# Forty-four modulation tiles moved to row products beside the up projections, and the inverse's transposes moved to VectorE

## The chip, the core and the metric

The kernel runs on one core of a Trainium2 chip. The metric is device time in microseconds (us): the median of several runs of the whole program. The engines are PE (TensorE), DVE (VectorE), ACT (ScalarE), POOL (GpSimd) and SP (SyncE, which issues most transfers); each works through its own list of instructions in order, and semaphores hold them to each other.

## What is computed

Two transformer-like blocks run one after the other on 256 tokens of width 1024, all in 32-bit floats. Cut to what matters here:

```python
def first_block(x, p, ...):                    # 256 x 1024
    z = rmsnorm(h) @ mix_w_in                  # layer 0
    y_a = rwkv7_bidir(z[..., :RWKV_COLS])      # 8 heads of 64, two directions, a recurrence over time
    y_b = hyena_bidir(z[..., RWKV_COLS:])      # long convolution by DFT products
    h = h + concat([y_a, y_b]) @ mix_w_out
    h = h + conv_ffn(h); h = h + per_layer_embedding(h)
    h = h + neighbourhood_attention(...)       # layer 1
    h = h + conv_ffn(h); h = h + per_layer_embedding(h)

def conv_ffn(h):
    u = dwconv_centred(rmsnorm(h) @ w_up, conv_w, conv_b)      # 1024 -> 2 x 2816
    return (gelu(u[..., :D_FF]) * u[..., D_FF:]) @ w_down

def second_block(x, c, ctx, c_ctx, w_mod, b_mod, ...):         # x is the first block's result
    for l in range(2):
        ml = split(silu(c) @ w_mod[l] + b_mod[l], 9)           # w_mod[l] is 1024 x 9216
        mc = split(silu(c_ctx) @ w_mod[l] + b_mod[l], 9)
        ...                                                    # half FFN, mixing, half FFN, modulated by ml, mc
```

The **modulation** of the second block depends on `c` and `c_ctx` alone, not on the first block: 2 layers x 9216 columns, for two conditions, that is 144 tiles of 128 columns (36 blocks of 512). It can be worked out at any time before the norms that use it.

## The kernel before

The stages follow each other on PE: in-projection of the first block (to about 121 us), hyena (121 to 167), the low-rank products of the RWKV ("lora", 167 to 187), its recurrence (187 to 369), the out-projection, the first conv FFN (up projection 408.6 to 560.8, down projection to about 633), embedding and neighbourhood attention, the second conv FFN (up projection from about 841), and from then on the second block (half00, mix0, half01, half10, mix1, half11).

**The modulation by PE.** 21 of the 36 blocks (all 18 of layer 0, the last three of layer 1) are computed as matrix products in small pieces that other stages let in. `tensor_modulation`, `scalar_modulation` and `vector_modulation` are generators; `Fill.to(n)` runs one of them up to step n, so that its instructions stand at that place of the engine's list. Block j takes two steps: step 2j+1 is the first eight products of 512 weights columns, step 2j+2 the second eight, with a small product ("columns", 128x4) that turns block j-1 ahead of them. The banks 2 and 3 of the PSUM alternate, so PE's step 2j+1 waits until DVE has done `add(j-2)` (L888), which stands in DVE's step 2j; PE's columns wait for a copy by ACT. Of the 43 steps 14 stand in the hyena (`HY_FILL` gives those between its DFT products: up to step 6, 8 and 12 after products 3, 5 and 7), two in the lora stage (`MOD_EARLY`, 16), and seven in each of the four recurrences (`fill_at`).

**The modulation by rows.** The other 60 tiles, all of layer 1, are computed by DVE without PE, 20 in each of half00, half01 and half10: a tile of 128 rows x 1024 of the transposed weights is loaded by an ACT queue (`scalar_rows_load`), and DVE multiplies it by silu(c) and silu(c_ctx) and adds up along the row, one instruction each (`vector_row`, L1354); `vector_rows_bias` adds the bias at the end. Two tile buffers alternate.

**The recurrence.** `tensor_scan`, `scalar_scan` and `vector_scan` run once for each of four pairs of heads, p = 0 to 3. In chunks of 64 steps the recurrence needs the inverse of a triangular matrix for eight units. It is built by doubling blocks, in levels 1 to 5 (block sizes 4 to 64): with `xi` the inverse so far and `xt` its transpose, PE computes p = et' xi, ACT copies it to `pk` (L1074), PE computes the correction dx = xt' pk and also dt = pk' xt, and DVE subtracts dx from xi (L1120) and dt from xt (L1124); level 5 has dt alone. Before level 1, xt is made by DVE (L1106), PE transposes it by products with the identity into bank `b0` ("xit"), and DVE copies that to xi (L1109). DVE fills its time between with the operands of the next pair, one piece in each level (`vector_prepare`, lines 730 to 775); p = 3 has no next pair. After the levels each p has a tail of products of the outputs and the state, with fills at points 13 to 18.

**The conv FFN.** `scalar_norm` lets ACT square the input, load the table with the logarithm (L269) and form 1/rms; `vector_norm` scales, and the up projection runs over 22 pairs (f) of column tiles of two halves: per half PE fills a bank, ACT takes the middle tap (`mid_tap`), DVE adds the outer two, and per f ACT's gelu and a DVE product end it. In the last four f DVE also forms sums of weights for the down projection (`vector_weight_sums`). `vector_fast` then forms the sums of activations (L1524) with which the down projection's fast scheme goes on.

All products of PE go through the helper at line 134; `sb_work`, `sb_big`, `sb_xn`, `sb_rope` are large on-chip buffers cut into areas, `weights` is a ring of four slots, `acc` and `aux` are four PSUM banks each.

## Time and profile before

| what | us |
|---|---|
| runs | 3063.7, 3064.5, 3067.2; median 3064.5 |
| span of the profiled execution | 3064.9 |
| PE busy | 2938.8 (96%) |
| DVE busy | 1524.0 (50%) |
| ACT busy | 594.4 (19%) |
| chain of waits, share of PE | 88% |

PE is busy nearly all the time, and it is also what the chain that ended last runs through: what leaves PE's list where PE is the bound is gained. The stages around the change are the exceptions to look into: between 121 and 370 us PE waits more often than elsewhere. A timeline row gives start and length in us, the engine, line, operation, the tiles out<-in, and how many records are put together; in brackets the idle time of the engine ahead of it and who ended it. One instruction of the program on a pair of halves shows as two records.

### The profile page before, as it was taken

What the parts mean: (1) busy time and instruction counts of PE and PEld (TensorE: products, weight loads), DVE (VectorE), ACT (ScalarE), POOL (GpSimd) and SP (SyncE); (2) the same over time, 40 slices, a digit from 0 to 9 for tenths busy, and PEclk for the clock granted to TensorE, in tenths of its full rate; (3) what the DMA queues carried; (4) which work ended last, traced back from release to release, by engine and by line L of the source; (5) the groups of instructions that cost most, each with busy time, mean ns of one, the idle gap of its engine ahead of it and who ended that gap; (6) DMA issues with size and microseconds to landing.
All of it is one profiled execution on the core that took longest, in us unless ns stands there. A gap on an engine that the chain in (4) does not pass through costs nothing.

```text
span 3064.9 us, 42878 instructions
## 1 busy us (share of the span) xinstructions
PE 2938.8 (96%) x17846; PEld 2394.0 (78%) x17846; DVE 1524.0 (50%) x3105; ACT 594.4 (19%) x1355; POOL 37.3 (1%) x60
## 2 busy tenths in 40 slices
PE   9988899999899999999999899999999999999999
PEld 7666788987588978888843448888878888765999
DVE  4266433532534556665313736666366673225675
ACT  1233222122422030100112621100020000224110
POOL 0000000020000000000000000000000000000000
PEclk9999999999999999999999999999999999999999
DMA  6644444465243544332303023332344322331444
GB/s 240 235 165 167 146 141 137 125 202 156 76 147 113 165 145 144 130 92 77 128 15 93 28 82 115 126 110 80 93 143 139 116 78 76 112 106 45 149 140 109
DMA packets 349316, 374.15 MB, mean 122 GB/s; under 512 B 8163, under 2 KB 282996, under 8 KB 348612
## 3 DMA queue, kind: packets, MB, share of 16 engines
q1 hardware_dynamic: 336228, 329.72, 34.3%
q10 hardware_dynamic: 10688, 36.38, 3.5%
q0 software_dynamic: 2208, 5.31, 0.9%
q8 instruction: 143, 2.34, 0.3%
q14 instruction: 49, 0.40, 0.0%
HBM read 370.34 MB, written 1.05 MB: 121 GB/s over the span
## 4 chain that ended last, share of the span: by engine, by line
PE 88%; DVE 6%; ACT 4%; issue 2%; DMA 0%; ACTq 0%; DVEq 0%
PE acc L134 74%; PE aux L134 13%; ACT sb_xn L280 1%; PE aux L2283 1%; ACT L269 0%; DVE sb_work L2009 0%; DVE sb_work L2006 0%; DVE sb_work L1519 0%; ACT sb_work L1808 0%; ACT sb_work L1810 0%; DVE sb_xn L258 0%; DVE sb_big L1120 0%; DVE sb_work L2020 0%; ACT sb_rstd L271 0%; DVE sb_work L1788 0%
## 5 line engine op out<-in xcount | busy, mean ns | idle before, releaser
L134 PE MATMUL acc<-sb_xn,weights 128*128 128x256 f32 (+2 forms) x5184 | 1215.6, 389 | 20.5 <-DVE sb_xn L258 12.2
L134 PEld LDWEIGHTS acc<-sb_xn,weights 128*128 128x128 f32 x5184 | 946.5, 191 | 243.8 <-issue 123.2
L134 PE MATMUL acc<-sb_work 128*128 128x256 f32 (+1 forms) x1944 | 374.7, 346 | 0.0
L134 PEld LDWEIGHTS acc<-sb_work 128*128 128x128 f32 x1944 | 324.3, 191 | 34.3 <-issue 0.4
L134 PE MATMUL acc<-sb_work,weights 128*128 128x256 f32 (+2 forms) x1508 | 322.5, 362 | 3.2 <-DVE sb_work L1257 1.4
L134 PE MATMUL acc<-sb_big,weights 128*128 128x256 f32 (+1 forms) x1776 | 315.4, 334 | 4.3 <-DVE sb_work L1667 4.0
L134 PEld LDWEIGHTS acc<-sb_big,weights 128*128 128x128 f32 x1776 | 279.7, 192 | 31.0 <-issue 5.7
L134 PEld LDWEIGHTS acc<-sb_work,weights 128*128 128x128 f32 x1508 | 254.5, 191 | 50.2 <-issue 21.8
L1487 ACT COPY sb_work<-acc 128x256 f32<-128x256 f32 (+1 forms) x112 | 37.9, 339 | 687.1 <-PE acc L134 687.1
L134 PE MATMUL aux<-sb_xn,sb_work 128*128 128x256 f32 (+1 forms) x704 | 152.2, 361 | 8.9 <-ACT sb_xn L280 8.9
L1557 DVE TENSOR_TENSOR sb_work<-sb_work,acc 128x256 f32<-128x256 f32 (+1 forms) x112 | 42.6, 380 | 226.5 <-PE acc L134 226.5
L1519 DVE TENSOR_TENSOR sb_work<-weights 128x512 f32<-128x512 f32 (+1 forms) x112 | 99.7, 890 | 95.2 <-PE acc L134 95.0
L1492 ACT ACTIVATE sb_work<-sb_work 128x256 f32<-128x256 f32 (+1 forms) x88 | 34.4, 391 | 570.7 <-DVE sb_work L1571 570.7
L134 PEld LDWEIGHTS aux<-sb_xn,sb_work 128*128 128x128 f32 x704 | 124.2, 195 | 24.3 <-issue 10.2
L1665 DVE SCALAR_TENSOR_TENSOR sb_work<-acc,sb_cols,sb_work 128x255 f32<-128x255 f32 x88 | 42.5, 482 | 187.3 <-ACT sb_work L1652 187.3
L134 PE MATMUL aux<-sb_big,sb_work 128*128 128x128 f32 (+3 forms) x592 | 110.9, 342 | 0.0
L1519 DVE TENSOR_TENSOR weights<-weights 128x512 f32<-128x512 f32 (+1 forms) x112 | 99.7, 890 | 3.1
L1519 DVE TENSOR_TENSOR sb_work<-sb_work,weights 128x512 f32<-128x512 f32 (+1 forms) x112 | 99.2, 886 | 2.6
L1599 DVE TENSOR_TENSOR sb_work<-sb_work,acc 128x256 f32<-128x256 f32 (+1 forms) x112 | 42.5, 379 | 116.2 <-PE acc L134 116.1
L1519 DVE TENSOR_TENSOR sb_work<-weights,sb_work 128x512 f32<-128x512 f32 (+1 forms) x112 | 99.1, 885 | 0.7
L134 PEld LDWEIGHTS aux<-sb_big,sb_work 128*128 128x128 f32 (+1 forms) x592 | 89.2, 186 | 10.9 <-issue 2.8
L1571 DVE TENSOR_TENSOR sb_work<-sb_work,aux 128x256 f32<-128x256 f32 (+1 forms) x112 | 42.4, 379 | 104.2 <-PE aux L134 104.2
(316 smaller groups left out, 2709.5 us busy)
## 6 DMA issues: line engine op xcount, KB each, us to landing
weights<-ffn_w_up SPq DMA_DIRECT2D x88, 1024.0 KB, 7.9
weights<-ffn_w_down SPq DMA_DIRECT2D x48, 1408.0 KB, 7.2
weights<-ffn_w_gate SPq DMA_DIRECT2D x44, 1024.0 KB, 5.4
weights<-w_mod SPq DMA_DIRECT2D x21, 2048.0 KB, 8.2
sb_work<-w_mod_rows ACTq DMA_DIRECT2D x60, 512.0 KB, 6.4
weights<-w_in SPq DMA_DIRECT2D x8, 2048.0 KB, 8.6
weights<-mix_w_in SPq DMA_DIRECT2D x6, 2048.0 KB, 12.7
weights<-na_w_qkv SPq DMA_DIRECT2D x6, 2048.0 KB, 10.8
```

The costliest lines, as they stand in the source:

```text
L134: return te.matmul(o, lhsT, rhs, start=start, stop=stop, skip_group_check=True)
L280: shifted.on(ac.activation(y, y, ACT.Identity, bias=N.shift(k, h)))
L1487: st_u.on(ac.copy(u[:, s, :], bank_a[:, 0:F.H]))
L1492: st_g2.on(ac.activation(g2[:, s, :], g2[:, s, :], ACT.Silu))
L1519: st_s.on(ve.tensor_tensor(to, one, other, op))
L1557: st_b.on(ve.tensor_tensor(u, u, bank_b[:, 0:F.H], ALU.add))
L1571: st_c12.on(ve.tensor_tensor(g2, g2, bank_e[:, 0:F.H], ALU.add))
L1599: st_c21.on(ve.tensor_tensor(u, u, bank_c[:, 0:F.H], ALU.add))
L1665: v_step.on(ve.scalar_tensor_tensor(u[:, 1:L], ps[:, 0:L - 1], cols("ffn_cw", 1, 132 * F.i + t), u[:, 1:L], ALU.mult, ALU.add))
L2283: ins_ = te.transpose(aux[u % 3][:, c:c + 128], mx_e[:, u % 4, W * i + 128 * kt:W * i + 128 * kt + 128], ident[:])
```

## The change

1. 11 of the 21 blocks leave PE: `MOD_BY_PE` keeps blocks 16 and 17 of layer 0 and 0 to 5, 16 and 17 of layer 1. Of the 21 steps left, two stand at the hyena's start and up to step 4 after its transposes, up to 9 after the last DFT product, 11 after the inverse, 13 in the lora stage, 14 to 16 ahead of the first recurrence, and one each of 17 to 21 in the recurrences (two in p = 3).
2. 44 more tiles go by rows: tiles 0 to 21 of layer 0 beside the first conv FFN's up projection, 22 to 43 beside the second's, with three tile buffers of their own. ACT issues the load of the conditions (1 MB) and of three tiles inside the norm, between the squares and the table load, after a wait for the whole input; it then takes the Silu and goes on as before, with a load in each f from 2 on. DVE does one row product per half and the bias after the last. The half FFNs keep 20 tiles each, now 44 to 63 of layer 0 and 24 to 63 of layer 1.
3. In the recurrence DVE transposes 32 x 32 blocks in place of PE: xi from xt before level 1 (the 32 small products of "xit" and the copy L1109 go), and xt from the new xi in levels 1 to 4 (dt's 16 instructions and the subtraction L1124 go). Up to there the inverse is zero outside of blocks of 32. Level 5 keeps dt.

The core of the diff:

```diff
+MOD_BY_PE = [(0, 16), (0, 17)] + [(1, b) for b in (0, 1, 2, 3, 4, 5, 16, 17)]
...
-    def scalar_norm(N):
+    def scalar_norm(N, between=None):
...
+        if between is not None:
+            between()
         ac.preload_act_table_set(NAT_LOG)
...
-    HY_FILL = {3: 6, 5: 8, 7: 12}
+    HY_FILL = {7: 9}
...
     def vector_hyena(other):
...
-        other.to(8)
+        other.to(4)
         ve.wait_ge(hy_spec.sem, hy_spec_at(7))
...
-        other.to(10)
+        other.to(6)
...
-        other.to(12)
+        other.to(9)
...
-    MOD_STEPS, MOD_EARLY = n_mod * 2 + 1, 16
+    MOD_STEPS, MOD_EARLY, MOD_FIRST = n_mod * 2 + 1, 13, 16
 
     def fill_at(p, point):
-        return min(MOD_STEPS, MOD_EARLY + 7 * p + point * 7 // 18)
+        return MOD_FIRST + (18 * p + point) * (MOD_STEPS - MOD_FIRST) // (18 * NP)
...
         other.to(fill_at(p, 2))
-        te.wait_ge(sc_xt.sem, sc_xt_at(p))
         te.wait_ge(sc_tm.sem, sc_tm_at(4 * p))
-        for u, hp, g, tt in UNITS:
-            for par in range(2):
-                ins_ = mm(b0[half(par), 64 * u:64 * u + 64], xt[half(par), u, :], ident[half(par), half(par)])
-        sc_xit.on(ins_)
...
                 sc_dx.on(ins_)
-            for u in range(8):
-                for par in range(2):
-                    ins_ = mm(aux[0][half(par), 64 * u:64 * u + 64], pk[half(par), u, :], xt[half(par), u, :])
-            sc_dt.on(ins_)
+            else:
+                for u in range(8):
+                    for par in range(2):
+                        ins_ = mm(aux[0][half(par), 64 * u:64 * u + 64], pk[half(par), u, :], xt[half(par), u, :])
+                sc_dt.on(ins_)
...
+        sc_xi.on(ve.transpose(wide(xi), wide(xt)))
         other.to(fill_at(p, 2))
-        ve.wait_ge(sc_xit.sem, sc_xit_at(p))
-        sc_xi.on(ve.tensor_copy(xi, blocks(b0[:])))
...
                 sc_xi.on(ve.tensor_tensor(xi, xi, blocks(aux[3][:]), ALU.subtract))
-            ve.wait_ge(sc_dt.sem, sc_dt_at(n))
-            if lv > 1:
+                ve.wait_ge(sc_xi.sem, sc_xi.n)
+                sc_xu.on(ve.transpose(wide(xt), wide(xi)))
+            else:
+                ve.wait_ge(sc_dt.sem, sc_dt_at(p))
                 ve.wait_ge(sc_xu.sem, sc_xu.n)
-            sc_xu.on(ve.tensor_tensor(xt, xt, blocks(aux[0][:]), ALU.subtract))
+                sc_xu.on(ve.tensor_tensor(xt, xt, blocks(aux[0][:]), ALU.subtract))
...
         for n, _ in enumerate(vector_prepare(0)):
-            if n == 1:
-                other.to(MOD_EARLY)
+            if n in (1, 2, 3):
+                other.to((MOD_EARLY, MOD_EARLY + 1, MOD_FIRST)[n - 1])
...
+    conv_cond, conv_tile = area(big, FT * L, 2, D), [area(big, FT * L + 2 * D + D * n, D) for n in range(3)]
...
-        scalar_norm(F.norm)
+        sig, value = F.norm.x_ready[KT - 1]
+        ac.wait_ge(sig.sem, value)
+        scalar_norm(F.norm, lambda: scalar_rows_begin(F.rows))
+        scalar_rows_cond(F.rows)
         for n, g in enumerate(F.groups):
             f, half = divmod(n, 2)
             t, u = f + half * FT, conv_u[:, f % 2, half, :]
+            if half == 0 and 2 <= f < ROWS_CONV - 1:
+                scalar_rows_load(F.rows, f + 1)
...
                     vector_weight_sums(F.fast, FT, (f - FT + 4,))
+            vector_row(F.rows, f, half)
+        vector_rows_bias(F.rows)
         vector_fast(F.fast, following=following)
```

PE's list in the hyena, from the DFT products of which two are left over (`aux<-sb_work 128x512`, two instructions each) to the inverse (`128x256 x16`); the products of weights are the modulation's steps, eight each, and `128x4 x2` its columns. Before:

```order
L134 MATMUL aux<-sb_work 128x512 x4
L134 MATMUL acc<-weights,sb_work 32x256 x8
L134 MATMUL acc<-sb_work,sb_rstd 128x4 x2
L134 MATMUL acc<-weights,sb_work 32x256 x8
L134 MATMUL aux<-sb_work 128x512 x4
L134 MATMUL acc<-weights,sb_work 32x256 x8
L134 MATMUL acc<-sb_work,sb_rope 128x4 x2
L134 MATMUL acc<-weights,sb_work 32x256 x16
L134 MATMUL acc<-sb_work,sb_rstd 128x4 x2
L134 MATMUL acc<-weights,sb_work 32x256 x8
L134 MATMUL aux<-sb_work 128x256 x16
```

Changed:

```order
L135 MATMUL aux<-sb_work 128x512 x16
L135 MATMUL acc<-weights,sb_work 32x256 x8
L135 MATMUL acc<-sb_work,sb_rope 128x4 x2
L135 MATMUL acc<-weights,sb_work 32x256 x16
L135 MATMUL acc<-sb_work,sb_rstd 128x4 x2
L135 MATMUL acc<-weights,sb_work 32x256 x16
L135 MATMUL aux<-sb_work 128x256 x16
```

The steps that stood between the DFT products are gone, and one run of steps stands between the last of these and the inverse, the last of them the first half of a block (step 9).

PE's list from the lora products (`aux<-sb_work 128x256`) over the norms of the first pair (`128x512`) to the first products of the recurrence (`64x128 x32`) and what follows them. Before:

```order
L134 MATMUL aux<-sb_work 128x256 x8
L134 MATMUL acc<-weights,sb_work 32x256 x8
L134 MATMUL acc<-sb_work,sb_rstd 128x4 x2
L134 MATMUL acc<-weights,sb_work 32x256 x8
L134 MATMUL aux<-sb_work 128x256 x4
L134 MATMUL acc<-sb_work,sb_blk 128x512
L134 MATMUL aux<-sb_work 128x256 x4
L134 MATMUL acc<-sb_work,sb_blk 128x512
L134 MATMUL aux<-sb_work 64x128 x32
L940 MATMUL acc<-sb_ident,sb_work 128x128 x8
L940 MATMUL aux<-sb_ident,sb_work 128x128 x8
L134 MATMUL acc<-sb_ident,sb_big 64x64 x16
```

Changed:

```order
L135 MATMUL aux<-sb_work 128x256 x8
L135 MATMUL acc<-sb_work,sb_rstd 128x4 x2
L135 MATMUL acc<-weights,sb_work 32x256 x16
L135 MATMUL aux<-sb_work 128x256 x4
L135 MATMUL acc<-sb_work,sb_blk 128x512
L135 MATMUL aux<-sb_work 128x256 x4
L135 MATMUL acc<-sb_work,sb_blk 128x512
L135 MATMUL acc<-sb_work,sb_rope 128x4 x2
L135 MATMUL acc<-weights,sb_work 32x256 x16
L135 MATMUL acc<-sb_work,sb_rstd 128x4 x2
L135 MATMUL acc<-weights,sb_work 32x256 x8
L135 MATMUL aux<-sb_work 64x128 x32
```

Step 13 now ends the run between the lora products 0 to 3 and 4 to 7, steps 14 to 16 stand ahead of the recurrence's first products, and the transposes "xit" (`acc<-sb_ident,sb_big 64x64 x16`) have no counterpart behind.

DVE's list at the start of the levels of p = 0 (the second row ahead of the first level's L743 is the xi copy, or the transpose in its place). Before:

```order
L1106 TENSOR_TENSOR sb_xn<-sb_big 128x512
L1109 COPY sb_big<-acc 128x512
L1115 TENSOR_TENSOR sb_xn<-sb_big 128x512
L743 SCALAR_TENSOR_TENSOR sb_work<-sb_work 128x256 x2
L745 TENSOR_TENSOR sb_work<-sb_work 128x512
L733 TENSOR_TENSOR sb_work<-sb_big 128x512
L736 SCALAR_TENSOR_TENSOR sb_work<-sb_work,sb_cols,sb_big 128x256 x2
L1120 TENSOR_TENSOR sb_big<-sb_big,aux 128x512
L1124 TENSOR_TENSOR sb_big<-sb_big,aux 128x512
L888 TENSOR_TENSOR sb_mod<-acc,sb_cols 128x2x2x2
```

Changed:

```order
L1108 TENSOR_TENSOR sb_xn<-sb_big 128x512
L1109 STREAM_TRANSPOSE sb_big<-sb_big 128x512
L1116 TENSOR_TENSOR sb_xn<-sb_big 128x512
L749 SCALAR_TENSOR_TENSOR sb_work<-sb_work 128x256 x2
L751 TENSOR_TENSOR sb_work<-sb_work 128x512
L739 TENSOR_TENSOR sb_work<-sb_big 128x512
L742 SCALAR_TENSOR_TENSOR sb_work<-sb_work,sb_cols,sb_big 128x256 x2
L1121 TENSOR_TENSOR sb_big<-sb_big,aux 128x512
L1123 STREAM_TRANSPOSE sb_big<-sb_big 128x512
L1116 TENSOR_TENSOR sb_xn<-sb_big 128x512
```

The number of DVE's instructions in a level stays; the copy from a bank and the second subtraction, which waited for PE, are transposes of what DVE itself has written just before.

## Rows read from the trace of the kernel before

**Rows 1.** Busy time by stage: stretch, length, PE, PEld, DVE, ACT, POOL, clock, DMA share, GB/s

```profile
187.60:370.00 182.40, 154.94 (x3846) 126.30 (x3847) 110.66 (x214) 50.23 (x106) 0.00 (x0) 0.98 0.45 152
408.00:561.00 153.00, 152.19 (x704) 133.84 (x704) 58.23 (x118) 34.86 (x67) 0.00 (x0) 1.00 0.42 130
```

**Rows 2.** Chain of waits in the hyena: start, length, engine, tile, line, count

```profile
136.44 2.54 PE acc L134 x36
```

**Rows 3.** Timeline, hyena: start, length, engine, line, operation, count, [idle before, releaser]

```profile
153.28 1.07 PE L134 MATMUL acc<-weights,sb_work 128*32 128x256 f32 x16 [1.96 <-DVE sb_mod L888]
```

**Rows 4.** Timeline, low-rank stage and the first recurrence's start

```profile
173.75 1.07 PE L134 MATMUL acc<-weights,sb_work 128*32 128x256 f32 x16
176.51 0.16 DVE L888 TENSOR_TENSOR sb_mod<-acc,sb_cols 128x8 f32<-128x8 f32 x1
183.64 0.69 DVE L766 TENSOR_TENSOR sb_work<-sb_work 128x512 f32<-128x512 f32 x1 [4.00 <-ACT sb_work L807]
187.64 3.69 PE L134 MATMUL aux<-sb_work 64*64 64x128 f32 x64 [6.82 <-DVE sb_work L774]
```

**Rows 5.** Timeline, third recurrence (p = 2): start and first level

```profile
283.59 1.98 PE L134 MATMUL aux<-sb_work 64*64 64x128 f32 x64 [1.15 <-DVE sb_work L1153]
289.21 0.68 DVE L1109 COPY sb_big<-acc 128x512 f32<-128x512 f32 x1
290.81 1.15 PE L134 MATMUL aux<-sb_big,sb_xn 64*64 64x64 f32 x32
292.73 1.10 PE L134 MATMUL aux<-sb_rope,sb_big 64*64 64x64 f32 x32
296.78 1.15 PE L134 MATMUL aux<-sb_big,sb_xn 64*64 64x64 f32 x32 [0.48 <-DVE sb_big L1120]
297.97 0.69 DVE L1115 TENSOR_TENSOR sb_xn<-sb_big 128x512 f32<-128x512 f32 x1 [0.58 <-PE aux L134]
```

**Rows 6.** Timeline, fourth recurrence (p = 3): three level starts, end of levels

```profile
336.97 1.15 PE L134 MATMUL aux<-sb_big,sb_xn 64*64 64x64 f32 x32
348.44 1.15 PE L134 MATMUL aux<-sb_big,sb_xn 64*64 64x64 f32 x32
352.21 1.15 PE L134 MATMUL aux<-sb_big,sb_xn 64*64 64x64 f32 x32
360.78 1.85 PE L134 MATMUL acc<-sb_xn,sb_big 64*64 64x128 f32 x29 [0.79 <-DVE sb_big L1124]
```

**Rows 7.** Chain of waits in the recurrence: fills, and a stall of issue

```profile
220.08 1.00 PE acc L134 x16
227.56 1.54 PE acc L134 x20
272.36 2.74 issue
```

**Rows 8.** Busy time in one stretch of level products (as Rows 1)

```profile
276.00:278.00 2.00, 2.00 (x31) 0.83 (x23) 0.75 (x2) 0.00 (x0) 0.00 (x0) 0.51 0.04 12
```

**Rows 9.** Timeline, first products of the two down projections

```profile
562.76 2.69 PE L134 MATMUL acc<-sb_big,weights 128*128 128x128 f32 x22 [2.00 <-DVE sb_work L1667]
997.25 4.21 PE L134 MATMUL acc<-sb_big,weights 128*128 128x128 f32 x22 [2.00 <-DVE sb_work L1667]
```

**Rows 10.** Timeline, DVE and PE just after the first up projection

```profile
564.31 1.62 DVE L1524 TENSOR_TENSOR sb_xn<-sb_big 128x1408 f32<-128x1408 f32 x1
566.07 2.69 PE L134 MATMUL acc<-sb_xn,sb_work 128*128 128x128 f32 x22 [0.62 <-DVE sb_xn L1524]
```

**Rows 11.** Timeline, what ACT issues and loads before a projection

```profile
838.72 1.28 ACT L269 ACT_TABLE_LOAD   x1
1110.08 1.03 ACTq L1335 DMA_DIRECT2D sb_work<-w_mod_rows  x2
```

**Rows 12.** Row products: busy, mean ns | idle; their loads: KB, us to landing

```profile
L1354 DVE SCALAR_TENSOR_TENSOR sb_work<-sb_work 128x1024 f32<-128x1024 f32 x60 | 73.1, 1218 | 0.1
sb_work<-w_mod_rows ACTq DMA_DIRECT2D x60, 512.0 KB, 6.4
```

More of the change, by code:

```diff
@@ L529, in tensor_hyena @@
             hy_inv.on(ins_)
-        other.to(14)
+        other.to(11)
     def vector_hyena(other):
@@ L556, in vector_hyena @@
             hy_out.on(ve.tensor_tensor(yb[:, ct, :], s_fm[:, ct, :], uhy[:, ct, :], ALU.mult))
-        other.to(14)
+        other.to(11)
     def scalar_hyena(other):
@@ L603, in scalar_lora @@
         wad_tanh.on(ac.activation(wad[0:64], wad[0:64], ACT.Tanh))
-        other.to(14)
+        other.to(11)
         for b in range(2):
@@ L700, in blocks, with wide @@
         return ap.rearrange("p (u t) -> p u t", u=8)
+    def wide(ap):
+        return ap.rearrange("p u t -> p (u t)")
     def quads(ap):
@@ L815, in tensor_prepare @@
         if p:
-            te.wait_ge(sc_xi.sem, sc_xi_at(5 * (p - 1)))
+            te.wait_ge(sc_tm.sem, sc_tm_at(4 * (p - 1)))
         q = t0 if p else dd
@@ L826, in tensor_prepare @@
         yield
-    mod_blocks = [(l, b, block(1, banks=(2, 3))) for l, b in [(0, b) for b in range(18)] + [(1, b) for b in range(BY_ROWS // 4, 18)]]
+    mod_blocks = [(l, b, block(1, banks=(2, 3))) for l, b in MOD_BY_PE]
     n_mod = len(mod_blocks)
@@ L1157, in tensor_recurrence @@
             pass
+        other.to(MOD_FIRST)
         for p in range(NP):
@@ L1165, in scalar_recurrence @@
             pass
+        other.to(MOD_FIRST)
         for p in range(NP):
@@ L1319, in build, with __init__ @@
     row_junk = area(big, 20 * T2, D)
+    conv_cond, conv_tile = area(big, FT * L, 2, D), [area(big, FT * L + 2 * D + D * n, D) for n in range(3)]
+    conv_junk = area(work, 3072, D)
     cond_in, cond_set = signal("row_condition_arrived", 16), signal("row_condition_set")
[L1321 removed]
+    rows_in, rows_done = [signal(f"mod_rows_arrived{n}", 16) for n in range(3)], signal("mod_rows_done")
     class ModRows:
[L1324 to L1325 removed]
+        def __init__(self, first, n=ROWS_EACH, cond=row_cond, tiles=row_tile, junk=row_junk):
+            self.first, self.n, self.silu_cond, self.tiles, self.junk = first, n, cond, tiles, junk
             self.cond, self.silu = cond_in.reserve(1)(0), cond_set.reserve(1)(0)
[L1327 to L1328 removed]
+            m = len(tiles)
+            at = [rows_in[i].reserve(len(range(i, n, m))) for i in range(m)]
+            self.arrived = lambda t: (rows_in[t % m], at[t % m](t // m))
             self.done = rows_done.reserve(2 * n)
     def scalar_rows_load(R, t):
[L1332 to L1333 removed]
+        m = len(R.tiles)
+        if t >= m:
+            ac.wait_ge(rows_done.sem, R.done(2 * (t - m) + 1))
         n0 = 128 * (R.first + t)
[L1335 removed]
+        rows_in[t % m].on(ac.dma_start(R.tiles[t % m], ins["w_mod_rows"][n0:n0 + 128, :]))
     def scalar_rows_begin(R):
[L1338 to L1339 removed]
+        cond_in.on(ac.dma_start(R.silu_cond.rearrange("p s k -> p (s k)"), ins["cond_rows"]))
+        for t in range(len(R.tiles)):
             scalar_rows_load(R, t)
@@ L1343, in scalar_rows_cond @@
         ac.wait_ge(cond_in.sem, R.cond)
-        cond_set.on(ac.activation(row_cond, row_cond, ACT.Silu))
+        cond_set.on(ac.activation(R.silu_cond, R.silu_cond, ACT.Silu))
     def vector_row(R, t, s):
@@ L1353, in vector_row @@
             ve.wait_ge(rows_done.sem, R.done(2 * t))
-        rows_done.on(ve.scalar_tensor_tensor(row_tile[t % 2] if s else row_junk, row_tile[t % 2], 1.0, row_cond[:, s, :],
-                                             ALU.mult, ALU.mult, accum_out=mod[:, 72 + R.first + t, s:s + 1]))
+        row = R.tiles[t % len(R.tiles)]
+        rows_done.on(ve.scalar_tensor_tensor(row if s else R.junk, row, 1.0, R.silu_cond[:, s, :],
+                                             ALU.mult, ALU.mult, accum_out=mod[:, R.first + t, s:s + 1]))
     def vector_rows_bias(R):
-        ve.wait_ge(rows_done.sem, R.done(2 * ROWS_EACH - 1))
-        m = mod[:, 72 + R.first:72 + R.first + ROWS_EACH, :]
-        v_step.on(ve.tensor_tensor(m, m, cols("b_mod", ROWS_EACH, 72 + R.first).unsqueeze(2).to_broadcast([128, ROWS_EACH, 2]), ALU.add))
+        ve.wait_ge(rows_done.sem, R.done(2 * R.n - 1))
+        m = mod[:, R.first:R.first + R.n, :]
+        v_step.on(ve.tensor_tensor(m, m, cols("b_mod", R.n, R.first).unsqueeze(2).to_broadcast([128, R.n, 2]), ALU.add))
     class Fast:
@@ L1628, in __init__ @@
             self.fast = Fast(CTX, up=False, hid_at=lambda f: (hid_set, hid(f)))
+            self.rows = ModRows(ROWS_CONV * i, ROWS_CONV, conv_cond, conv_tile, conv_junk)
             self.x_ready = self.fast.x_ready
@@ L2706, in layout @@
     arrays["w_ukv"] = np.concatenate([flat(ukv[..., 0:NOPE]), flat(ukv[..., NOPE:])], axis=-1)
-    arrays["w_mod_rows"] = a["w_mod_2"][1].T[0:128 * BY_ROWS]
+    arrays["w_mod_rows"] = a["w_mod_2"].transpose(0, 2, 1).reshape(DEPTH * 9 * D, D)
     arrays["cond_rows"] = np.broadcast_to(np.concatenate([a["c_ctx_2"].reshape(-1), a["c_2"].reshape(-1)]), (128, 2 * D))
```

24 lines of the change are left out of this document (7 added, 17 removed).

## The prediction

> **What bounds the kernel now.** I read the chain of waits first, then busy time by stage, then the timeline of PE and DVE. PE is busy 96% of the span and carries 88% of the chain, so an instruction that leaves PE is gained only where nothing else ends last. In the recurrence PE is busy 154.9 of 182.4 us and DVE 110.7; in an up projection PE 152.2 of 153.0 and DVE 58.2 [rows 1]. So the row products go where DVE is two thirds idle, and what they replace leaves a stage in which PE and DVE take turns: part of that work fills PE's waits today. In the first level of p = 2 PE's next product waits for DVE's L1120, not for PE's own list [rows 5]; in p = 3, where DVE prepares nothing, level follows level at PE's pace [rows 6]. So p = 0 to 2 are bound by DVE in levels 1 to 4, p = 3 by PE throughout.
>
> **The change part by part**, against the profiled span of 3064.9, which is 0.4 over the median.
>
> *Hyena.* Two groups of two steps between the DFT products are on the chain, 2.54 each, the first of them shown [rows 2]: **-5.1**. What is left, steps 5 to 9 after the last DFT product, has a new wait. Step 9 needs `add(2)`, which DVE now does only after the spectrum product that also releases the inverse. Before, such a wait for L888 cost 1.96 in this place [rows 3]. The inverse then waits for an add (0.16), some 0.3 of hand-over and a step of 1.07 [rows 4], less what the other steps covered: **+1.2**, and +0.2 for step 11 behind the last output product.
>
> *Low-rank stage.* Step 13 stood free at 173.75. Now it needs `add(4)`, which on DVE is queued behind the pieces of `vector_prepare(0)` where before an add stood at 176.51; PE comes to it at about 176.8, and behind it in PE's list stand the lora products 4 to 7 and the norm of p = 0. ACT reads these, and DVE waits 4.00 for ACT at 183.64 [rows 4], so all of it is on the path: **+3.0**. Steps 14 to 16 lie in the 6.82 that PE waits ahead of the recurrence and cost nothing there (1.54 each at most, rows as in [rows 7]). They keep PE busy: the first products took 3.69 after that wait, 1.98 in p = 2 [rows 4, 5]. Gain 0 to 1.7; I take **-0.5**, since PE still waits some 3 us there.
>
> *Starts of the recurrences.* The copy L1109 begins at 289.21 and level 1 at 290.81, behind fills and the product it waits for [rows 5]. DVE's transpose can start where the copy did (the row before it on DVE is the same) and takes, as I assume, the copy's 0.68: level 1 at 289.95, a gain of 0.85. In p = 3 the same reckoning gives 0.2. **-2.3** for four. No row shows a DVE transpose. Its bounds are 0.16, the shortest DVE row here [rows 4], and 1.218 for 1024 columns, the longest of one pass [rows 12]; I take 0.68, a copy of the same tile. The Trainium skill's "Vector Engine (DVE) Microarchitecture Reference", section 3.8 "The reshape front-end and per-opcode configuration", says the transpose mode sustains one element per cycle per lane, the rate of a plain copy; no run here shows it.
>
> *Levels 1 to 4 of p = 0 to 2.* PE loses dt (1.10), DVE swaps a subtraction for a transpose. After L1120 DVE has L1124 (0.68), then waits 0.58 for PE's product before L1115 [rows 5]; so the transpose is hidden up to about 1.2 us. The cycle of L1120, p, L1115 and the pieces of the next pair remains: **0**.
>
> *Levels of p = 3.* They took 360.78 - 336.97 = 23.8. One without a fill took 352.21 - 348.44 = 3.77 [rows 6]. Without dt PE could be faster still, but p, ACT's copy, dx and the subtraction follow each other in any case; 5 x 3.77 = 18.9. **-4.9**.
>
> *Level 5 and the tails of p = 0 to 2.* Nine fills of 1.00, 1.54 or (one) 1.76 are on the chain, 11.9 in all, the first two shown [rows 7]. Three of the new steps, some 3.0 together, come back there; of the other 8.9 a third is lost again because the copy or the subtraction behind a fill is late next: **-5.8**. A stall of issue of 2.74 on the chain [rows 7] follows a stretch in which the fills' loads saturate the transfers; their loads are gone: **-2.7**.
>
> *PE's clock.* After that stall the level products ran at a granted clock of 0.51, that is at 1.2 GHz [rows 8], and 22 products took 4.21 instead of 2.69 after an idle time of 2.00 that in the other down projection left the clock alone [rows 9]. Of eight idle times of 1.6 to 2.8 us in this trace, five show such a fall. Taking fills and dt away makes more: from the end of dx (292.73 + 1.10) to 296.78 PE had dt and a fill, and now has nothing for 2.9 us [rows 5]. I count twelve such turns of levels (four in each of p = 0 to 2) and four tails. A level product at 1.2 GHz costs 1.1 more (1.15 to 2.2). PE's slowness falls on the path in the turn of p, and partly under DVE's pieces in that of dx. Five eighths of 16 is 10, at 0.7 each: **+7** (0 to 17.6).
>
> *Up projections.* DVE: 58.2 + 44 x 1.218 [rows 12] = 111.8 of 153 us, and PE gives 152.2/22 = 6.92 per f for the two products. A tile lands in 6.4 [rows 12], three are in flight: hidden. Ahead of the table load ACT now issues four transfers, two of which took 1.03 [rows 11]: about 2. In the first conv FFN most lies under the wait for the last square, +0.7; in the second the table load at 838.72 [rows 11] is on the chain, +1.5. At the end the last row product (1.22) and the bias stand ahead of L1524, for which PE waits at 566.07 [rows 10]: +1.5 twice. **+5.2**, and **+1.5** (0 to 3.4) for the clock, since PE's idle 2.00 there grows [rows 9].
>
> **Sum**: -5.1 + 1.4 + 3.0 - 0.5 - 2.3 - 4.9 - 5.8 - 2.7 + 7 + 5.2 + 1.5 = -3.2. 3064.9 - 3.2 - 0.4 = 3061.3, so **3061**.
>
> **The rivals.**
>
> *The clock holds.* If nearly all 16 gaps are too short to lower it (as after the 2.00 of 562.76 [rows 9]), the +7 and the +1.5 go: 3061.3 - 8.5 = 3053. For it: three of eight gaps had no fall, and the gaps here recur with products between. Against: five of eight had.
>
> *Every gap lowers it* (the slower side). Then the twelve turns and four tails cost 1.1 each, 17.6 instead of 7: 3061.3 + 10.6 = 3072. The rest of the sum is -10.2, so this is slower than before from 10 us of clock cost, and clearly so from 17. For it: [rows 8], where a whole stretch stays low after one gap. The Trainium skill, "TensorE: Matmul & The Clock Gate", section "A second HAM failure mode: psum-queue depth-cycling", describes this: a TensorE that idles briefly between groups of products often enough swings between its two levels, and the loss is between the products rather than in them. The trace agrees in that the fall is at 272 us, after idle time between groups, not in a long run of products.
>
> *The transpose is slow.* At T us it costs 16 x (T - 1.2) in the levels and 4 x (T - 0.68) at the starts. At 1.8 that is 14: 3075. Slower than before from about 1.26, by more than can be told from no change from 1.56. For it: no row shows the operation; against: DVE's rows of 512 columns took 0.68 or 0.69, whatever they did [rows 4, 5].
>
> *The tails give it back.* If the nine fills only lie where DVE or ACT is next late by as much, -5.8 becomes -1: 3066.
>
> **How the numbers follow.** Forecast 3061 (its own range 3057 to 3066): 0.57. Clock holds, 3053 (3048 to 3057): 0.27. Every gap lowers it, 3072: 0.06. Slow transpose, 3075: 0.05. Tails give back, 3066: 0.05. The range 3050 to 3068 leaves out a fifth of the second case (0.05) and the two slow ones (0.11). A measurement of this kernel tells about 0.2%, 6.1 us, from no change: faster means below 3058.4, slower above 3070.6. Faster: the second case and a fifteenth of the first, 0.31; slower: the two slow cases less their near ends, 0.09; same: the rest, 0.60.
>
> **What would show it.** After: no steps between the DFT products, the inverse waiting a step longer; lora products 4 to 7 about 3 us later against the first ones; level 1 about 0.7 behind the copy's old place; STREAM_TRANSPOSE near 0.68; levels of p = 3 at 3.8 each, those of p = 0 to 2 as before (the first of p = 2 took 296.78 - 290.81 = 5.97 [rows 5]); the granted clock of the recurrence below the 0.98 of now [rows 1], with level products of 2.2 instead of 1.15; an up projection of 152.2, with its start and its end about 1.5 later against the stages around. The prediction is wrong where the transpose takes over 1.3, where the clock doesn't fall or falls throughout, where the recurrence is held by ACT instead, or where a row product ends later than its f.

## The result, and the profile after

The changed kernel takes **3067.3 us** (median of 20 runs, 3063.6 to 3071.1) against 3063.5 before (20 runs, 3059.3 to 3067.2). The ratio is 1.0014, 95% interval 1.0008 to 1.0020: some 4 us slower, where 3 us faster was forecast. By the forecast's bound of 0.2% it counts as the same; the time lies inside the range, but it went the other way. Runs of one kernel differ by some 8 us, and a profile is one of them; so kernels are compared by their medians, and profiles stage by stage.

The page of the changed kernel: busy time, and the granted clock in 40 slices of 77 us.

```profile
PE 2910.4 (95%) x16810; PEld 2375.2 (78%) x16810; DVE 1624.5 (53%) x3272; ACT 596.8 (19%) x1348; POOL 37.3 (1%) x60
...
PEclk9988899999999999999999999999999999999999
```

PE lost 28 us of busy time, DVE gained 100, and the time did not fall. The 8s in the clock line stand where the recurrences are. Busy time by stage (stretch, length, PE, PEld, DVE, ACT, POOL, granted clock, DMA share, GB/s): p = 0, 1 and 2, then the first up projection, which answer to [rows 1].

```profile
187.00:234.40 47.40, 32.70 (x700) 27.06 (x701) 32.01 (x60) 12.56 (x26) 0.00 (x0) 0.82 0.16 60
234.40:281.10 46.70, 32.74 (x704) 27.23 (x705) 30.99 (x57) 12.85 (x27) 0.00 (x0) 0.81 0.15 47
281.10:329.70 48.60, 32.45 (x704) 27.78 (x704) 30.91 (x56) 12.55 (x26) 0.00 (x0) 0.82 0.01 2
...
404.00:557.00 153.00, 152.18 (x704) 133.67 (x704) 106.72 (x204) 37.89 (x69) 0.00 (x0) 1.00 0.62 209
```

The granted clock of the recurrences was 0.98 over all four before; in three of them it is now 0.81 or 0.82, as a mean of stretches at 2.4 and at 1.2 GHz. In the up projection the row products are hidden, as forecast: DVE 106.7 (111.8 worked out), PE 152.2 as before.

PE's timeline in p = 0, first level to second, with the end of the levels:

```profile
193.50 1.15 PE L135 MATMUL aux<-sb_big,sb_xn 64*64 64x64 f32 x32 [2.56 <-DVE sb_big L1109]
194.45 1.13 PE L135 MATMUL acc<-sb_xn,sb_big 64*64 64x64 f32 x32
195.38 1.13 PE L135 MATMUL aux<-sb_rope,sb_big 64*64 64x64 f32 x32
199.45 1.97 PE L135 MATMUL aux<-sb_big,sb_xn 64*64 64x64 f32 x32 [2.94 <-DVE sb_big L1121]
201.35 2.07 PE L135 MATMUL acc<-sb_work,sb_blk 128*128 128x512 f32 x2
203.36 1.97 PE L135 MATMUL aux<-sb_rope,sb_big 64*64 64x64 f32 x32
...
222.24 3.46 PE L135 MATMUL acc<-sb_xn,sb_big 64*64 64x128 f32 x29 [0.79 <-DVE sb_big L1127]
```

Where dt and a fill stood [rows 5], PE waits 2.94 for DVE; the next product takes 1.97 instead of 1.15, and the ones behind it are as slow. The granted clock of that stretch is 0.50, that is 1.2 instead of 2.4 GHz:

```profile
198.70:205.50 6.80, 5.88 (x66) 4.07 (x66) 5.19 (x11) 2.21 (x4) 0.00 (x0) 0.50 0.00 1
```

PE stays there for several groups, not for one. The product behind the levels takes 3.46 where p = 3 of before took 1.85 [rows 6].

DVE at the same place:

```profile
192.69 0.70 DVE L1109 STREAM_TRANSPOSE sb_big<-sb_big 128x512 f32<-128x512 f32 x1
...
198.72 0.68 DVE L1121 TENSOR_TENSOR sb_big<-sb_big,aux 128x512 f32<-128x512 f32 x1
199.43 0.71 DVE L1123 STREAM_TRANSPOSE sb_big<-sb_big 128x512 f32<-128x512 f32 x1
201.47 0.69 DVE L1116 TENSOR_TENSOR sb_xn<-sb_big 128x512 f32<-128x512 f32 x1 [1.32 <-PE aux L135]
```

A transpose takes 0.70 to 0.71 (0.68 was assumed), and DVE then waits 1.32 for PE's slow product: it is not the transpose that holds the turn.

By stage, from the start of the first row of each to that of the next (us). The last column is the same stage in an experiment below that takes the cause away, or holds the clock by dead products. The hyena is an exception: no edit touches it, and the clock simply held there in e3, e7 and e8 (26.76 or 26.77); with the same instructions it took 28.1 to 29.8 in e2, e5, e6 and e10.

| stage | before | changed, two profiles | cause removed or clock held |
|---|---|---|---|
| hyena, transposes to inverse | 31.07 | 28.23, 27.62 | 26.76 (e7) |
| lora products 0 to 3, to 4 to 7 | 5.54 | 8.61, 9.47 | 4.55 (e5) |
| from there to the recurrence | 12.89 | 12.89, 14.75 | 12.89 (e5), 14.74 (e8) |
| p = 0 | 46.32 | 47.34, 48.71 | 43.71 (e8) |
| p = 1 | 49.63 | 46.72, 46.88 | 42.79 (e8) |
| p = 2 | 46.80 | 48.55, 48.44 | 42.92 (e8), 45.36 (e6) |
| p = 3, to the out-projection's second half | 58.08 | 53.87, 53.69 | 52.30 (e8) |
| to the first up projection | 20.11 | 20.66, 20.65 | 20.11 (e10) |
| up to down projection, wait and sums | 3.31 | 4.81, 4.81 | 3.43 (e7) |
| first down projection | 77.45 | 79.07, 79.07 | 77.44 (e7) |
| neighbours to the second up projection | 165.53 | 166.78, 166.76 | 165.42 (e8) |
| second up projection | 155.65 | 155.76, 155.85 | 154.18 (e8) |
| up to down projection, wait and sums | 3.99 | 4.80, 4.72 | 3.42 (e8) |
| second down projection | 77.54 | 79.08, 79.07 | 77.45 (e8) |

Other stages come out at one of a few lengths, in kernels with and without the change, and what decides it isn't shown: the embedding at 32.55 or 34.24, the norm of half00 at 40.6 or 42.3. A fall in mix1, which this profile of before has and none of the other eleven, makes the two spans look equal (before, then changed, the same products):

```profile
2769.63 4.07 PE L134 MATMUL acc<-sb_big 64*128 64x512 f32 x8
```

```profile
2772.43 2.19 PE L135 MATMUL acc<-sb_big 64*128 64x512 f32 x8
```

### The profile page after: what moved, and what is told of

Its sections match the earlier page's. It is cut to its first block, busy times and chain, and to the rows that moved or that the text cites. A ratio compares the mean times of both kernels' runs of the same rounds, so it can differ in the third digit from the quotient of the medians.

```text
span 3064.1 us, 40978 instructions
## 1 busy us (share of the span) xinstructions
PE 2910.4 (95%) x16810; PEld 2375.2 (78%) x16810; DVE 1624.5 (53%) x3272; ACT 596.8 (19%) x1348; POOL 37.3 (1%) x60
## 4 chain that ended last, share of the span: by engine, by line
PE 88%; DVE 6%; ACT 4%; issue 1%; DMA 0%; ACTq 0%; DVEq 0%
PE acc L135 74%; PE aux L135 13%; ACT sb_xn L283 1%; PE aux L2301 1%; ACT L272 0%; DVE sb_big L1121 0%; ACT sb_work L1826 0%; DMA weights<-mix_w_in 0%; ACT sb_work L1828 0%; DVE sb_work L1529 0%; DVE sb_work L2027 0%; DVE sb_work L2024 0%; DVE sb_big L1101 0%; PE aux L1950 0%; DVE sb_work L1806 0%
## 5 line engine op out<-in xcount | busy, mean ns | idle before, releaser
L135 PE MATMUL acc<-sb_xn,sb_work 128*128 128x128 f32 (+1 forms) x528 | 93.7, 336 | 4.2 <-DVE sb_xn L1534 4.2
```

What stands on the lines that cost most here:

```text
L135: return te.matmul(o, lhsT, rhs, start=start, stop=stop, skip_group_check=True)
```

## The experiments

**Theory**: the change removes work from PE where DVE sets the pace; the idle time lowers PE's clock, and the products that are on the path then take nearly twice as long. **Rivals**: DVE's transposes lengthen the levels; the loss lies in the hyena, the lora stage and the ends of the up projections alone. Times are medians; "before" is from the same chip and hours.

**The changed kernel again** (e0), for a second profile.

> The changed kernel once more, for a second profile and for times on the same chip as the three below. Theory (clock falls in PE's idle times, some in every execution, some in part of them): the recurrences p = 0 to 2 take 141 to 144 us again at a granted clock of 0.80 to 0.84; stages that follow one idle time (the down projections, the embedding, the norm before half00) come out at one of two lengths 1.6 to 1.7 apart, not always the same as in the first profile. 3064 to 3069.

3067.0 (12 runs), ratio 1.0011 (1.0002 to 1.0021). p = 0 to 2 take 144.0 at 0.81 to 0.82 again, both down projections 79.07 again, and the embedding, 34.24 in both, and the norm of half00 (42.40 after 40.66) show the two lengths. The falls in the recurrence and behind the up projections come in both profiles.

**Transposes alone** (e1): the kernel before with part 3 of the diff and nothing else.

> The kernel before with part 3 of the change alone: DVE transposes in the recurrence, all 21 modulation blocks on PE at their old places. Theory (the idle time that PE gets in p = 0 to 2 lowers its clock): the old fills still stand in most turns, so the granted clock of p = 0 to 2 falls only part of the way, to 0.88 to 0.96, against 0.95 to 1.00 before and 0.82 changed; the starts give 2 to 3 us, p = 3 some 3 to 4, and the time is 3056 to 3061 beside 3063.5 before. Rival (DVE's transposes themselves lengthen the levels, or the turns end on something else): the clock is as before and p = 0 to 2 are no shorter or longer, 3062 to 3066.

3061.4 (12 runs), ratio 0.9995 (0.9987 to 1.0004): no difference. The granted clock of p = 0 to 2 is 0.91, 0.86 and 0.93, between before (0.95, 0.97 and 1.00) and changed, and p = 0 and 2 are 0.1 and 0.3 shorter than before, p = 1 1.5 longer: the stages gain nothing. p = 3 gives 1.6, less than the 3 to 4 expected. In time it lies between the two expectations, in the clock near the theory, with p = 1 below its range.

**Rows alone** (e2): the changed kernel with part 3 taken back.

> The changed kernel with PE's transposes put back (xit and dt as before): parts 1 and 2 alone. Theory (clock): dt fills a third of each turn's idle time, so the granted clock of p = 0 to 2 is 0.86 to 0.95, and p = 0 to 2 together take 138 to 141 us against 142.6 changed; p = 3 is 2 us or so longer than changed; the up projections cost what they cost in the changed kernel (the boundary to the down projection 4.8 instead of 3.3). In all 3062 to 3067. Rival (what the change lost lies in hyena, low-rank stage and up projections, not in the recurrence): p = 0 to 2 as long as changed or longer, over 3067.

3063.0 (12 runs), ratio 0.9998 (0.9990 to 1.0007). In its profile, which is of the slowest of the twelve (3071.2), p = 0 to 2 take 45.26, 44.42 and 49.45 at 0.93, 0.95 and 0.81: 139.1 in all, within the range, and the stage follows its clock; p = 3 is 1.1 longer than changed, not 2. The boundary is 4.81. Neither part alone loses measurably, both together lose 4: with fills (e1) or with dt (e2) PE's clock stays above 0.85 in five of six stages, without either it is 0.81 or 0.82 in all six of two profiles.

**Dead products** (e3): products that nobody reads, put where PE waits.

```diff
         te.wait_ge(sc_tm.sem, sc_tm_at(4 * p))
+        if p + 1 < NP:
+            ... 16 products of the identity with itself into b0
...
                 sc_dx.on(ins_)
+                for _ in range((2 if lv == 1 else 1) if p + 1 < NP else 0):
+                    ... 16 products of pk with itself into aux[0]
```

> The changed kernel with dead products on PE in p = 0 to 2, whose results nobody reads: one group of 16 ahead of level 1, two after dx of level 1, one after dx of levels 2 to 4, each as long as dt (about 1 us). Nothing waits for them; they only fill PE's idle time. Theory (clock): the granted clock of p = 0 to 2 rises from 0.82 to 0.93 or more and the three take 133 to 137 us instead of 142.6, so that the time is 3058 to 3062 beside 3067.3. Rival (PE's idle time costs nothing by itself; the turns are bound by DVE and ACT): the lengths stay at 142 to 144 or grow by the dead products' time, 3067 to 3071.

In its profile p = 0 to 2 take 44.63, 42.46 and 45.39, 132.5 instead of 142.6, by doing more work on PE. Busy time of p = 1 and 2, and PE's timeline of p = 1 (start, level 1 with the dead products behind dx, level 2, level 5, end of the levels, start of p = 2):

```profile
233.90:276.30 42.40, 31.85 (x896) 28.07 (x897) 30.89 (x57) 12.82 (x27) 0.00 (x0) 1.00 0.16 52
276.30:321.70 45.40, 35.71 (x892) 31.47 (x893) 30.81 (x56) 12.51 (x26) 0.00 (x0) 0.88 0.01 3
```

```profile
233.86 1.98 PE L135 MATMUL aux<-sb_work 64*64 64x128 f32 x64 [1.14 <-DVE sb_work L1164]
...
240.24 1.15 PE L135 MATMUL aux<-sb_big,sb_xn 64*64 64x64 f32 x32 [1.43 <-DVE sb_big L1117]
...
243.09 2.03 PE L135 MATMUL aux<-sb_rope 64*64 64x64 f32 x64
246.21 1.15 PE L135 MATMUL aux<-sb_big,sb_xn 64*64 64x64 f32 x32 [1.09 <-DVE sb_big L1129]
...
263.29 1.15 PE L135 MATMUL aux<-sb_big,sb_xn 64*64 64x64 f32 x32 [0.84 <-DVE sb_big L1129]
...
267.06 1.85 PE L135 MATMUL acc<-sb_xn,sb_big 64*64 64x128 f32 x29 [0.79 <-DVE sb_big L1135]
...
276.32 3.21 PE L135 MATMUL aux<-sb_work 64*64 64x128 f32 x64 [1.14 <-DVE sb_work L1164]
```

At a clock of 1.00 the whole recurrence step takes 42.46. But the median of the runs is 3065.7: they fall into two groups, five of 3053 to 3059 and seven of 3065 to 3074, the first at a mean clock of 0.987 to 0.989, the second at 0.981 to 0.985. The median lies between the two expectations; the first group is as fast as the theory said or faster, most of the second as slow as the rival said or slower. The profile is of a run of the first group. Idle time was left in the tails and after level 4, and the last row shows a fall behind a tail in the profile too. Why a run falls into one group or the other the one trace doesn't show.

**More dead products** (e6): with step 13 moved (e5, next), a second group after level 4 of p = 0 and 2, half groups in the waits of the tails, one group ahead of the next recurrence.

> The changed kernel with step 13 moved as in e5 and dead products as in e3, and more of them: a second group after dx of level 4 in p = 0 and 2, half groups in the waits of the tails and one group ahead of the next recurrence. Theory (clock): p = 0 to 2 take 128 to 131 us (p = 1 of e3 took 42.5 at a clock of 1.00), the granted clock there is over 0.96, and the runs no longer fall into two groups; 3050 to 3054. Rival (dead products end up on the path, in the tails above all): p = 0 to 2 as in e3 or longer, 3056 to 3062.

**3048.7** (6 runs, 3043.4 to 3051.4), ratio 0.9949 (0.9934 to 0.9963). One group of runs; p = 0 to 2 take 43.71, 42.83 and 45.36 at 1.00, 0.96 and 0.92. It is a little faster than expected, and 131.9 missed the expected 131 by a little, since a fall was left in the tail of p = 2. The three stages are hardly shorter than in e3's profile (132.5), which is of the faster of its two groups; what is new is that the runs form one group. The cleanest comparison is with e5 (next), from which e6 differs by the dead products alone. p = 0 to 2 together, e5 and then e6, in the columns used above:

```profile
184.50:327.00 142.50, 95.95 (x2104) 81.21 (x2105) 93.65 (x172) 37.91 (x77) 0.00 (x0) 0.84 0.12 41
183.20:315.10 131.90, 107.75 (x2984) 95.84 (x2985) 93.84 (x172) 37.91 (x77) 0.00 (x0) 0.96 0.13 46
```

PE is busy 11.8 longer, DVE and ACT do the same work in the same time, the granted clock rises from 0.84 to 0.96, and the stages are 10.6 shorter; the ratios to before are 0.9992 and 0.9949, some 13 us apart. The theory holds, and its rival (the dead products end up on the path) falls.

**Step 13 later** (e5): one number, and DVE's steps with it.

```diff
-    MOD_STEPS, MOD_EARLY, MOD_FIRST = n_mod * 2 + 1, 13, 16
+    MOD_STEPS, MOD_EARLY, MOD_FIRST = n_mod * 2 + 1, 12, 16
...
-                other.to((MOD_EARLY, MOD_EARLY + 1, MOD_FIRST)[n - 1])
+                other.to((MOD_EARLY, 14, MOD_FIRST)[n - 1])
```

> The changed kernel with step 13 of the modulation taken from between the lora products to the run ahead of the first recurrence (MOD_EARLY 12 instead of 13). Theory (step 13's wait for an add queued behind DVE's mixes is on the path): lora products 4 to 7 start at once, about 3 us earlier, and the first recurrence with them, 2 to 3 us; 3064 to 3065.5 beside 3067.3. Rival (ACT's exponentials or DVE's pieces end last there anyway): the first recurrence starts as late as in the changed kernel within 0.5 us, 3067.

3060.1 (11 runs), ratio 0.9992 (0.9981 to 1.0002). PE in the lora stage of the changed kernel, then of e5:

```profile
173.16 1.07 PE L135 MATMUL acc<-weights,sb_work 128*32 128x256 f32 x16 [3.00 <-DVE sb_mod L894]
174.17 1.13 PE L135 MATMUL aux<-sb_work 64*128 64x256 f32 x8
...
187.06 1.98 PE L135 MATMUL aux<-sb_work 64*64 64x128 f32 x64 [2.11 <-DVE sb_work L780]
```

```profile
171.62 1.13 PE L135 MATMUL aux<-sb_work 64*128 64x256 f32 x8
...
184.51 1.98 PE L135 MATMUL aux<-sb_work 64*64 64x128 f32 x64 [1.29 <-DVE sb_work L780]
```

The wait of 3.00 for the add is gone, and from the first lora products to the recurrence it is 17.44 instead of 21.50: 4.1, the wait and the step itself. The whole kernel gains 6 to 7, more than the 2 to 3 expected; where the rest comes from isn't shown. The rival falls.

**Rows off the ends** (e7): the loads are issued after the norm, and both products of a tile stand in the first half of its f.

```diff
-        scalar_norm(F.norm, lambda: scalar_rows_begin(F.rows))
+        scalar_norm(F.norm)
+        scalar_rows_begin(F.rows)
...
-            vector_row(F.rows, f, half)
-        vector_rows_bias(F.rows)
+            if half == 0:
+                vector_row(F.rows, f, 0)
+                vector_row(F.rows, f, 1)
+                if f == FT - 1:
+                    vector_rows_bias(F.rows)
```

> The changed kernel with the row products taken off both ends of the up projections: ACT issues the loads after the norm instead of inside it, and DVE does both products of a tile in the first half of its f, so that the last ones and the bias stand ahead of the last taps. Theory (the loads and the last product are on the path): the time from the out-projection to the up projection 20.1 instead of 20.7, neighbours to the second up projection 165.4 instead of 166.8, the boundary to the down projection 3.3 to 3.6 instead of 4.8, and the down projections 77.5 instead of 79.1 where the shorter wait no longer lowers the clock: 5 to 8 us in all, 3060 to 3063 beside 3067.3. Rival (later loads hold up ACT and so the first banks): the up projection itself longer than 154.1 by what is gained.

3057.6 (12 runs), ratio 0.9982 (0.9970 to 0.9993). The boundary behind the first up projection, changed and then e7:

```profile
558.27 2.69 PE L135 MATMUL acc<-sb_big,weights 128*128 128x128 f32 x22 [1.89 <-DVE sb_work L1683]
563.08 3.19 PE L135 MATMUL acc<-sb_xn,sb_work 128*128 128x128 f32 x17 [2.12 <-DVE sb_xn L1534]
```

```profile
558.76 2.69 PE L135 MATMUL acc<-sb_big,weights 128*128 128x128 f32 x22 [2.00 <-DVE sb_work L1684]
562.19 2.69 PE L135 MATMUL acc<-sb_xn,sb_work 128*128 128x128 f32 x22 [0.73 <-DVE sb_xn L1534]
```

The wait for the sums falls from 2.12 to 0.73, and the down projection behind it from 79.07 to 77.44. The start of the first up projection stays at 20.65, so it wasn't the loads there. In the second up projection it was: there ACT's four issues keep it from the table load.

```profile
838.70 1.55 ACTq L1344 DMA_DIRECT2D sb_big<-w_mod_rows  x3
840.29 1.28 ACT L272 ACT_TABLE_LOAD   x1 [1.56 <-issue]
```

The up projection is not longer (154.18 and 154.26), so the rival falls. The median is 9 us below the changed kernel's, where 5 to 8 were expected. The profile is of the fastest run (3052.3); the six stages from the boundary on give 10.1 in the profiles, of which some 2, in the neighbourhood attention, are not the edit's: e7 has 163.53 there and e8 165.42.

**All three** (e8): e7's edit on e6.

> Step 13 moved, dead products as in e6 and the rows off the ends as in e7. Theory: the gains add, since they lie in different stages: 3044 to 3050, faster than both kernels. Rival (the clock falls elsewhere instead): 3054 or more.

**3042.3** (6 runs, 3038.4 to 3043.6), ratio 0.9930 (0.9916 to 0.9945): faster than both kernels, by 0.7% than before, and a little faster than expected. Busy time of p = 0 to 2 in its profile, which is of the fastest run:

```profile
183.20:226.90 43.70, 34.78 (x1012) 30.65 (x1009) 31.18 (x57) 12.85 (x27) 0.00 (x0) 1.00 0.23 84
226.90:269.70 42.80, 35.47 (x980) 31.82 (x981) 30.98 (x57) 12.88 (x27) 0.00 (x0) 0.96 0.16 52
269.70:312.60 42.90, 34.93 (x1007) 30.75 (x1007) 30.90 (x56) 12.47 (x26) 0.00 (x0) 1.00 0.01 3
```

Against the changed kernel that is 25 us; by the ratios some 6 come with e5's step, 13 with the dead products and 6 with e7's edit. So the rival that puts the whole loss outside the recurrence is half right: the clock of the recurrence is the larger part, not the only one.

**Without ACT's wait for the input** (e10): e8 without the two lines that wait for `x_ready[KT - 1]` ahead of the squares.

> e8 without ACT's wait for the whole input ahead of the norm's squares (with the loads after the norm nothing needs it). Theory (that wait, not the issuing of the loads, makes the first up projection start later: e7 left 20.66 as it was): from the out-projection to the up projection 20.1 instead of 20.66, all else as in e8; 3041 to 3042. Rival (the wait is hidden and the 0.55 has another cause): 20.66 again.

The stage is 20.11 again, as in the kernel before: it was that wait, which holds the squares back until the last eighth of the input is there. The time is 3042.4 (5 runs), no different from e8: 0.55 can't be told in it.

**The kernel before with dead products** (e9), a control.

```diff
+        if p == 0:
+            te.wait_ge(pd_clamp.sem, pd_clamp_at(0))
+            dead(b0, 6)
...
+        if p + 1 < NP:
+            dead(b0, 1)
```

> The kernel before, with dead products where PE waits there: six groups ahead of the first recurrence (after the norm of p = 0 has been read) and those of e6 in the tails of p = 0 to 2. A control: is the gain of e6 and e8 one of dead products alone? Theory (the dead products only give back what the change opened; before, fills and dt kept PE busy): the first recurrence's first products take 1.98 instead of 3.69, p = 0 44.6 instead of 46.3, the rest unchanged; 3059 to 3062. Rival (PE's clock held the kernel before back as much): 3050 to 3056.

3068.9 (12 runs), ratio 1.0018 (1.0009 to 1.0027): slower, and both expectations missed. The first products take 1.98 as expected, but p = 0 is 46.43 all the same: it reaches level 1 in 6.36 instead of 8.24, and its tail takes 12.99 instead of 11.01, with the dead products on the path beside the fills. There are more stalls of issue: 2.64 in p = 1, and in p = 3, which has no dead products and still grew from 58.08 to 64.40, 1.03 and one of 2.83, shown here with the busy time ahead of it and in it.

```profile
366.00:369.80 3.80, 3.80 (x176) 3.66 (x172) 1.59 (x6) 1.03 (x3) 0.00 (x0) 1.00 0.98 320
369.80:372.70 2.90, 0.07 (x3) 0.04 (x2) 0.06 (x1) 0.00 (x0) 0.00 (x0) 0.74 0.22 75
```

So dead products gave nothing by themselves here; in the kernel before the clock of p = 0 to 2 was 0.95 to 1.00 and left little to give back. They pay where the change has opened idle time. Why p = 3 has more stalls isn't shown.

## Why the prediction was wrong

The step that failed is **PE's clock in the recurrence**: the mechanism was named, and its size was wrong. I counted gaps (16), took ten falls and charged each with 0.7 of a microsecond; 6.6 of the 7 lie in p = 0 to 2. The number of falls was about right: the granted clock of the changed kernel falls nine times in these three stages, in both profiles. What was wrong is the price of one. A fall lasts over several groups: at a mean of 0.82, some 51 of the 142.6 us are at the lower level (worked out from the mean), the level products behind a fall run at 1.2 GHz one after the other, and a tail that begins so costs about 2 (p = 0: 12.16 against 10.35 in e3; p = 2: 11.93 against 9.72 in e8). Against e8 (129.4) the changed kernel's 142.6 pays 13.2, not 6.6, some 1.5 for each fall; against e6 and e10, the same stages with a fall left in the tail of p = 2, it is 10.7 and 10.4. The rival in which every gap lowers the clock priced this better (17.6) than the forecast did, though by more falls than came, and by level products of 2.2 that take 1.97.

Point by point, where the clock held (e3, e8) unless another is named:

- **Starts**: from a recurrence's first product to level 1, p = 2 took 7.22 before [rows 5] and 6.37 in e8: -0.85 for -0.85, with the transpose at 0.70. But that price held for p = 2 alone; p = 1 and p = 3 went from 6.58 to 6.38. Together about -1.4 for the -2.3 (and 3 x 0.85 + 0.2, as it was put, would be 2.75).
- **Levels 1 to 4 of p = 0 to 2**: from the first to the fifth p product 23.05 in e3 (240.24 to 263.29) and 23.05 before (290.81 to 313.86, p = 2). Zero was right, as long as the clock holds; in the changed kernel p = 1 took 27.25.
- **Levels of p = 3**: 337.46 to 356.36 in the changed kernel, 18.90 for the 18.9 worked out from [rows 6]. Right.
- **Level 5 and tails of p = 0 to 2**: together 12.59 and 38.85 before, 11.33 and 29.63 in e8, which is 10.5 with the stall of issue and 7.7 without its 2.74. Predicted was 5.8: too small. Less was lost behind the fills than the third that I took off. The tails differ: p = 0 gave 0.5, p = 2 gave 2.8. PE in p = 2, from the end of the levels to the next recurrence, before (with the start of level 5), changed and e8:

```profile
313.86 1.15 PE L134 MATMUL aux<-sb_big,sb_xn 64*64 64x64 f32 x32 [0.84 <-DVE sb_big L1120]
317.88 1.85 PE L134 MATMUL acc<-sb_xn,sb_big 64*64 64x128 f32 x30 [0.79 <-DVE sb_big L1124]
...
330.39 1.98 PE L134 MATMUL aux<-sb_work 64*64 64x128 f32 x64 [1.15 <-DVE sb_work L1153]
```

```profile
317.74 3.46 PE L135 MATMUL acc<-sb_xn,sb_big 64*64 64x128 f32 x29 [0.79 <-DVE sb_big L1127]
...
329.67 3.69 PE L135 MATMUL aux<-sb_work 64*64 64x128 f32 x64 [1.14 <-DVE sb_work L1156]
```

```profile
302.86 1.85 PE L135 MATMUL acc<-sb_xn,sb_big 64*64 64x128 f32 x29 [0.79 <-DVE sb_big L1142]
...
312.58 1.98 PE L135 MATMUL aux<-sb_work 64*64 64x128 f32 x64 [0.21 <-DVE sb_work L1171]
```

- **Stall of issue**: the 2.74 is gone in both profiles of the changed kernel; e1 and e9, which keep the loads of 11 blocks, have 2.06 and 2.64 in p = 1. Right.
- **Lora**: +3.07 for +3.0, and e5 shows the cause. Right. Steps 14 to 16 were meant to keep the clock up for the first products: 1.98 for 3.69 in both profiles of the changed kernel, 1.7 for the 0.5 taken, but 3.69 again in e3 and e7. p = 0 grew by what came after.
- **Hyena**: -2.84 and -3.45 for -3.9. The forecast sum is right when the clock holds (26.76, -4.3); in the changed kernel's profile it falls where PE waits for the add, and the steps before the inverse run at 1.2 GHz. The same wait of 1.96 left the clock alone in e3, e7 and e8.

```profile
147.25 1.74 PE L135 MATMUL acc<-weights,sb_work 128*32 128x256 f32 x16 [1.96 <-DVE sb_mod L894]
148.92 1.02 PE L135 MATMUL acc<-sb_work,sb_rstd 128*128 128x4 f32 x4
149.87 3.64 PE L135 MATMUL acc<-weights,sb_work 128*32 128x256 f32 x32
```

- **Up projections**: starts +0.55 and +1.25 for +0.7 and +1.5, the first by ACT's wait and not by the loads; boundary +1.5 for +1.5. Hidden row products: right. Their clock was priced too low: behind the wait of 2.12 (0.62 before, [rows 10]) each down projection is 1.6 longer, and behind the longer wait ahead of the second up projection that one is 1.6 longer than in e1 and e9 (154.19 and 154.21; in its own profile the kernel before has a fall there too), 4.7 in all for the 1.5 taken.
- **Idle times with a fall**: the prediction's "five of eight" is not what the whole trace of before has. It has 18 waits of PE of 1.6 to 2.8 us, and nine or ten of them show a fall. The share taken was a little high, which does not explain the miss.

The misses come to +1.1 (hyena), +4.4 (p = 0 to 2, by e8: 6.6 more clock, 2.2 more gain), +0.5 (p = 3) and +2.8 (up and down projections), 8.8 against the 7 between forecast and result; the rest isn't traced to a stage. That the time still lies inside the range is in part luck: gain and clock cost of the recurrence were both put too low, and the one hid part of the other.

Of the rivals, the slow transpose is out (0.71), and so is the one in which the tails give the gain back. "The clock holds" is out as it stands, since the clock fell. In its terms, 3061.3 - 8.5, less the +3.0 and +5.2 that e5 and e7 take away, would be 3044.6; e8, which takes both away and holds the clock with dead products, measured 3042.3.

## What to carry to other kernels

When work leaves an engine that waits for another, ask what that work kept going. Here PE's fills and the redundant dt in levels 1 to 4 cost nothing on the path (23.05 with and without them). Without them and the fills of the tails, three stages lost some 13 us to the clock, all that the change gained there; dead products in the waits gave it back. Price a fall of the clock by how long the following stage stays slow, read from such a stage in a trace, and not by one product behind the gap. A step with a wait is best put where nothing queues behind it, and work for an idle engine ends one piece before the stage does.
